# The first expert's rows from a product in SBUF instead of a store, a gather and transposes

## The reference

```python
h = rmsnorm(x, norm2_g[l]) * (1 + scale2) + shift2
x = x + gate2 * hier_moe(h, ...)
# hier_moe, on t = h as 320 rows of 2048:
g_prob = softmax(t @ w_rg + b_rg); g_top, g_idx = top_k(g_prob, 1)        # one of 4 groups
e_top, e_idx = top_k(softmax(e_logits of that group), 2)                   # two of its 4 experts
hid = silu(einsum("td,edf->tef", t, w_gate)) * einsum("td,edf->tef", t, w_up)
out = einsum("tef,efd->td", hid * gates, w_down)
...
```

## Time and profile before

| | |
|---|---|
| median of 3 runs | 1379.21 us (1378.17 to 1382.27) |
| the profiled execution, device time | 1379.37 us |
| its span, first to last instruction | 1377.6 us |
| TensorE matmuls busy | 1188.9 us, 86% |
| VectorE, ScalarE, GpSimd busy | 300.3, 197.1, 96.6 us |
| DMA moved | 401.10 MB |
| mean granted TensorE clock | 0.933 of full |

### The profile page before, as it was taken

The page is one execution under the profiler, slowest core; times in us unless marked ns, Lnnn a source line. Parts: engine busy times, 40 slices in busy tenths (PEclk is TensorE's granted clock), DMA queues, the critical chain, the costliest instruction groups (busy, mean ns, idle before and its releaser), DMA issues.

```text
span 1377.6 us, 15972 instructions
## 1 busy us (share of the span) xinstructions
PE 1188.9 (86%) x6320; PEld 643.5 (47%) x6321; DVE 300.3 (22%) x634; ACT 197.1 (14%) x384; POOL 96.6 (7%) x126
## 2 busy tenths in 40 slices
PE   2688999999999999999998279989997998899830
PEld 0235656665545445544545235544553454445420
DVE  0111220222112214213112701210211111111128
ACT  2002101011121222010101001111111011101102
POOL 2010000000000000100000000000010000000016
PEclk8778999989999999999999589999999999999975
DMA  9997877844674645852633268999999999999953
GB/s 323 422 365 265 333 288 274 345 191 185 259 291 183 253 177 215 297 221 89 238 126 122 94 225 305 403 419 414 383 410 408 420 370 425 408 379 385 424 205 105
DMA packets 71718, 401.10 MB, mean 291 GB/s; under 512 B 6489, under 2 KB 6713, under 8 KB 39645
## 3 DMA queue, kind: packets, MB, share of 16 engines
q1 hardware_dynamic: 63216, 368.59, 67.7%
q0 software_dynamic: 6864, 23.47, 5.0%
q10 hardware_dynamic: 1600, 8.50, 1.7%
HBM read 394.85 MB, written 17.22 MB: 299 GB/s over the span
## 4 chain that ended last, share of the span: by engine, by line
PE 70%; DMA 22%; DVE 5%; issue 1%; ACT 1%; SPq 0%; POOLq 0%; DVEq 0%
PE bank L804 20%; DMA arena<-in_w_gate_dram 12%; PE bank L881 10%; PE bank L1152 8%; PE bank L1149 6%; PE bank L799 5%; PE bank L808 5%; PE bank L1175 4%; DMA arena<-in_w_ada_dram 4%; DMA arena<-in_w_up_dram 4%; PE bank L1172 2%; DMA arena<-in_w_in_dram 2%; PE bank L825 1%; PE bank L899 1%; PE bank L1135 1%
## 5 line engine op out<-in xcount | busy, mean ns | idle before, releaser
L804 PE MATMUL bank<-arena 128*128 128x512 f32 x640 | 287.4, 600 | 0.0
L1149 PE MATMUL bank<-arena 128*64 128x256 f32 x1536 | 175.1, 386 | 27.8 <-DMA arena<-in_w_gate_dram 15.1
L804 PEld LDWEIGHTS bank<-arena 128*128 128x128 f32 x640 | 118.9, 191 | 136.6 <-issue 135.4
L1149 PEld LDWEIGHTS bank<-arena 128*64 128x64 f32 x1536 | 110.2, 138 | 96.6 <-DMA arena<-in_w_gate_dram 20.5
L881 PE MATMUL bank<-arena 128*128 128x320 f32 x512 | 142.4, 438 | 3.9 <-DMA arena<-in_w_in_dram 3.9
L799 PE MATMUL bank<-arena 128*32 128x512 f32 x768 | 102.9, 678 | 43.7 <-DMA arena<-in_w_ada_dram 32.2
L1152 PE MATMUL bank<-arena 128*128 128x512 f32 x256 | 117.0, 619 | 16.8 <-DMA arena<-in_w_gate_dram 9.3
L881 PEld LDWEIGHTS bank<-arena 128*128 128x128 f32 x512 | 97.4, 192 | 50.8 <-issue 7.3
L1172 PE MATMUL bank<-arena 128*64 128x512 f32 x384 | 85.1, 595 | 6.0 <-DVE arena L1632 6.0
L1152 PEld LDWEIGHTS bank<-arena 128*128 128x128 f32 x256 | 50.5, 199 | 82.8 <-issue 70.9
L1629 DVE SCALAR_TENSOR_TENSOR arena<-bank,arena 128x512 f32<-128x512 f32 x16 | 12.0, 750 | 318.4 <-PE bank L1149 188.9
(11 more groups left out here) (310 smaller groups left out, 809.8 us busy)
## 6 DMA issues: line engine op xcount, KB each, us to landing
arena<-in_w_ada_dram SPq DMA_DIRECT2D x48, 2048.0 KB, 14.7
arena<-in_w_gate_dram SPq DMA_DIRECT2D x32, 2048.0 KB, 21.2
arena<-in_w_up_dram SPq DMA_DIRECT2D x32, 2048.0 KB, 21.9
arena<-in_w_down_dram SPq DMA_DIRECT2D x32, 2048.0 KB, 21.3
arena<-in_w_in_dram SPq DMA_DIRECT2D x20, 2048.0 KB, 7.8
arena<-in_w_out_dram SPq DMA_DIRECT2D x8, 2048.0 KB, 9.0
arena<-mod_final POOLq DMA_DIRECT2D x6, 1024.0 KB, 11.7
arena<-expert_rows SPq DMA_DIRECT2D x8, 512.0 KB, 7.7
```

The lines of the kernel that those rows point to most:

```text
L804: return mm(bank[:, :], lhsT=xT_[:, t, OFF[j]:OFF[j] + P], rhs=w, start=start, stop=stop)
L1149: last = mm(PB[bank][64 * h:64 * h + 64, 0:HALF], lhsT=XeT[:, t0 + t, 0:64], rhs=slots_w[slot][:, t, HALF * h:HALF * h + HALF], start=star ...
```

## The change

The rows of expert 0 are no longer gathered from DRAM. TensorE multiplies `h2p`, as stationary operand in 16 strided slices of 128 columns, by `Pm` of expert 0, over the three token tiles, into the same four PSUM banks that the transposes filled: 16 x 3 matmuls. The product of a slice of `h` and the place matrix is that slice of `XeT`, so nothing has to be transposed. The rows are still stored to DRAM, for the gathers of the other experts. Since `Pm` is read by the product until its end, `pick(1)`, which overwrites it, moves behind the product's end. ScalarE now waits for the three stores itself before its loop, since the buffers that the loop writes lie over `h2p`. `transpose_rows` counts gathers from one less. GpSimd issues `gather(1)` without a gather before it.

```diff
@@ gpsimd
             for k in range(3):
                 pool.wait_ge(h2_stored[k], 16)
-            pool.wait_ge(idx_ready, 1)
-            gather(0)
             pool.sem_inc(Ye_free, 1)
             pool.wait_ge(tables, 1)
...
             pool.wait_ge(idx_ready, 2)
-            pool.wait_ge(XTp, 4)
             gather(1)
...
-            pool.wait_ge(Xe_in, 16 * NE * passes + 32)
+            pool.wait_ge(Xe_in, 16 * NE * passes + 16)
@@ scalar
             act.sem_inc(Ye_s, 1)
+            for k in range(3):
+                act.wait_ge(h2_stored[k], 16)
             with act.Fori(0, passes) as p:
@@ tensor
             def transpose_rows(i):
-                pe.wait_ge(Xe_in, 16 * i + 16)
+                pe.wait_ge(Xe_in, 16 * i)
...
             slot_info(0, 0)
+
+            pe.wait_ge(x1T_out, 12)
+            pe.wait_ge(h2_ready, 3)
+            for k in range(4):
+                for c in range(4):
+                    for j in range(3):
+                        n = NT[j]
+                        last = mm(PB[2 + k][:, P * c:P * c + P], lhsT=h2p[j][0:n, 4 * k + c::KT], rhs=Pm[0:n, j, :], start=(j == 0), stop=(j == 2))
+                last.then_inc(XTp, 1)
             pe.wait_ge(tables, 1)
             passes = pe.value_load(nit[0:1, 0:1].bitcast(I32), min_val=1, max_val=PASSES)
-            transpose_rows(0)
             slot_info(1, 1)
@@ vector
+            xt_out(0)
+            dve.wait_ge(XTp, 4)
             pick(1)
-            xt_out(0)
             indices(1)
             pick(2)
```

## The result

The changed kernel takes 1395.17 us in the median of 4 runs (1394.10 to 1395.68), the kernel before, on the same chip, 1379.71: a ratio of 1.0109, with an interval of 1.0092 to 1.0127. It is slower by 15.5 us. The forecast was no change, 1378.5, and the time lies outside the range. One run each of two variants further down was far longer (1455.94 and 3195.11 us); the medians count it, the ratios leave it out.

A forecast was written before the change was run, and what follows sets the result against it. The first expert's start was taken to bound the kernel: 15.45 us freed, 13.15 spent on product, semaphore and tail, 1.10 on `pick(1)`, some 0.4 on semaphores and weight loads, winning 0.8, so 1378.5 us; range 1373.5 to 1382.0.

The forecast's parts named there:

- What bounds the kernel: When the first expert starts (801.59 us) sets the weight stream, so a microsecond won or lost before it moves the end equally.
- What is removed: Between the last modulated tile and `slot_info(1)`, the store's wait, gather and transposes leave the path, freeing 15.45 us.
- The third token tile has 64 rows instead of 128; I count it in full: In the product, the 64-row tile was priced like full ones: 96 passes of 0.111 us, 10.7 us at full clock.
- The stride costs nothing that I can see: In the product, strided `h2p` slices were priced at no extra cost, from transposes at 0.226 us a pass at half clock.
- The clock: In the product, the clock was to rise after 3.46 to 5.40 us, making it 12.4 to 13.4 us, middle 12.9.
- the rival that was given 0.05: The clock does not rise during the product: 96 passes take 21.3 us, end at 1386.9 us; chance 0.05.
- `pick(1)`: Moved behind the product, it was to run from 791.25 to 792.35 us, adding 1.10 us that had been hidden.
- The head of the loop: From `slot_info(1)` to the first expert, order and prices were to stay: 8.45 us, with a gap of about 6 us.
- neither rival about it: Shifted code makes the wait before the first expert cheaper (1373.5 us, chance 0.13) or dearer (1383.0 us, chance 0.09).
- The sum: The first expert moves from 801.59 to about 800.8 us, winning 0.8 us (0.3 to 1.3), so 1378.5 us in all.

## Why the prediction was wrong, step by step

- **What bounds the kernel: right.** The 16.76 us by which the first expert starts later came through to the end (16.4 of the span). (The description of the kernel before is off in one point: from 755 to 802 us VectorE is busy for 29.16 of 47 us, with the routing and the modulated tiles; the other engines are idle most of the time.)
- **What is removed: right.** The gather and the transposes are gone, and the store is waited for by nothing on the path.
- **"The third token tile has 64 rows instead of 128; I count it in full": the step that failed.** Counting it in full seemed the safe side. It was the cheap side: the changes between 128 and 64 rows cost 0.59 us in each of 16 groups, about 9.4 in all, in 7.2 of which the weight load stands idle, and with these pauses the clock did not rise. By the runs with contiguous slices, 64 rows against 128 are worth 16.7 us (30.01 against 13.28).
- **"The stride costs nothing that I can see": failed too.** It was read from transposes, which do not pay for it (0.113 at full clock), and an ordinary matmul with the same operand does (0.215 at full clock; 0.22 for the product at either clock). It is nearly hidden here, since the clock stays low anyway; without the changes of rows it costs 7.9 us. Each of the two faults is enough to lose: with either mended alone the product takes 21.1 or 30.0 us, with both 13.2.
- **The clock: the rival that was given 0.05 came about**, for another reason than the one named there, and the changes of rows put 9 us on top of its 21.3. A warm start does not help.
- **`pick(1)`: right**, 1.10 forecast, 1.16 measured alone, and 808.50 to 809.58 in after.
- **The head of the loop: as forecast here**, 6.46 us of issue as before (6.70), so neither rival about it took place. That the gap depends on where the code lies was right: with 92 places more, or in the two other kernels with 192 places more than after, it is 0.55; that the 160 places of the change do not cure it is seen from after. That it is late code agrees with the packets, and is not shown beyond that.
- **The sum.** With contiguous slices of full height the forecast's sum is met: 1377.53 us with a product of 13.18. In after the first expert is 17.6 us later than forecast; 17.3 of that are the product, and the rest is mostly `slot_info(1)`, which now runs at half clock (1.46 us for 0.58).

What stays open is why a change of rows idles the load for 0.22 us, why the clock does not rise with these pauses, and why transposes are exempt from the stride (the profile does not tell which of its two operands a transpose loads). The runs show that it is so, and not the mechanism.

## What to carry to other kernels

Price a matmul by a row that has its operation, its operand's step and its neighbours' rows: a transpose and a matmul of like shape differ by a factor of two on a strided operand. Don't let 128-row and 64-row tiles alternate; where the other operand holds zeros and the rows beyond hold finite numbers, take the full height. Where an engine waits for "issue" at a loop's head while an instruction packet arrives, a few instructions more or less ahead of it can be worth more than the change itself, so compare such kernels at several places of the code.

## What the runs showed of the hardware that was not expected

- An fp32 pass with a 128-column load takes 0.112 us at full clock with operand steps of 1 column, 0.118 with 2, and 0.22 to 0.23 with 4, 8 and 16 (the 16 in another run); with 16 it takes 0.22 at half clock too.
- Going between loads of 128 and of 64 rows costs about 0.3 us each way (half of 0.59), and a product with such a change every two to four passes stayed at 1.2 GHz for all of its 30 us; begun at 2.4 GHz it was at 1.2 after 0.87 us and stayed there.
- 92 places more of code, in matmuls without use, made this kernel 7.9 us faster, 0.57%: the wait at the loop's head went from 6.70 to 0.55 us. The Trainium skill, "Runtime: NRT & Kernel Launch", section "Instruction fetch mechanics", says that a taken branch to code outside the two blocks at hand must wait for a fetch; that the last packet comes at 786 to 788 in the kernel without the gap, and at 798 to 800, within the gap, in the other, agrees with it.
